# Threshold search of a top-256 selection: bits carried in the threshold, 32 steps written out, six blocks on ScalarE

## The reference, cut to what matters

```
dots  = einsum('bqhe,bke->bqhk', qi, ki)                # 4 index heads of width 64
score = einsum('bqh,bqhk->bqk', wi, relu(dots))
score = where(kpos // 64 <= qpos // 64, score, -1e30)
_, sel = top_k(score, 256)                              # ties: the earlier key wins
...
s = einsum('bqhd,bqjd->bhqj', q, k[sel]) * d**-0.5 + bias
p = softmax(where(valid, s, -1e30))
```

## Time and profile before

| | us |
|---|---|
| runs before, median (lowest, highest) of 3 | 4577.51 (4568.18, 4579.27) |
| profiled execution, time | 4576.58 |
| its span | 4574.8 |
| granted TensorE clock, mean of the span | 0.925 of full |
| TensorE busy in the span | 3894.7 (85%) |
| VectorE busy | 2334.4 (51%) |
| ScalarE busy | 1540.0 (34%) |
| counts of L2329 on VectorE, 340 instructions | 397.8 |
| sign passes of L2369 on ScalarE, 160 instructions | 303.2 |
| matmuls of this stage (cd_pA) | 264.7 + 245.1 |
| rank scans of L2409, 15 instructions | 42.4 |

### The profile page before, as it was taken

One profiled execution on the slowest core, in us unless ns is written; L12 is line 12 of the kernel. 1 busy time (PEld: TensorE's weight loads), 2 busy tenths in 40 slices (PEclk: granted clock), 3 DMA queues, 4 the chain that ended last, 5 costly groups with the idle time before them and its releaser, 6 DMA issues. The chain is left out here.

```text
span 4574.8 us, 52424 instructions
## 1 busy us (share of the span) xinstructions
PE 3894.7 (85%) x18129; PEld 2678.9 (59%) x18129; DVE 2334.4 (51%) x5034; ACT 1540.0 (34%) x2330; POOL 676.9 (15%) x408
## 2 busy tenths in 40 slices
PE   5999999968887999996988787789666489999798
PEld 3789989956664656565856433334344355555376
DVE  6211111157764544532310889999655677766422
ACT  3101001124433343333300778770233233333332
POOL 3100000012112111103400000000111432211133
PEclk9999999989997999998999898889778689999899
DMA  5222122143325222305411111011311311000243
GB/s 185 62 73 73 63 72 70 65 106 87 79 56 107 61 65 65 70 1 185 156 67 52 43 60 46 32 53 62 104 42 44 79 45 32 23 24 5 84 145 131
DMA packets 222646, 328.50 MB, mean 72 GB/s; under 512 B 22240, under 2 KB 129176, under 8 KB 221040
## 3 DMA queue, kind: packets, MB, share of 16 engines
q1 hardware_dynamic: 162768, 216.87, 16.8%
q10 hardware_dynamic: 54432, 91.91, 5.4%
q0 software_dynamic: 5216, 16.70, 1.7%
HBM read 214.42 MB, written 110.99 MB: 71 GB/s over the span
## 5 line engine op out<-in xcount | busy, mean ns | idle before, releaser
L2329 DVE TENSOR_SCALAR_CACHE_REDUCE cd_junk<-score,cd_thr 128x384 bf16<-128x384 f32 (+7 forms) x340 | 397.8, 1236 | 0.1
L1102 DVE TENSOR_REDUCE attB_mx<-attB_p_s 128x1 f32<-128x512 f32 (+2 forms) x360 | 211.2, 608 | 324.4 <-PE attB_p_s L949 207.8
L497 DVE COPY ab_stage<-ab_pA 128x256 f32<-128x256 f32 (+1 forms) x108 | 56.4, 523 | 602.7 <-PE ab_pA L466 572.6
L2369 ACT ACTIVATE cd_scratch<-score,cd_less 128x1664 bf16<-128x1664 f32 (+4 forms) x160 | 303.2, 1895 | 72.4 <-DVE cd_less L2348 67.0
L369 PE MATMUL cd_pA<-hT_cd,cd_W 128*128 128x512 f32 (+1 forms) x640 | 264.7, 578 | 73.4 <-ACT cd_stage L2475 60.9
L464 PE MATMUL ab_pA<-ab_W_hi,h_hi 128*128 128x256 f32 x1088 | 309.0, 284 | 3.2 <-PE ab_pA L466 3.1
L465 PE MATMUL ab_pA<-ab_W_lo,h_hi 128*128 128x256 f32 x1088 | 307.9, 283 | 0.0
L466 PE MATMUL ab_pA<-ab_W_hi,h_lo 128*128 128x256 f32 x1088 | 307.8, 283 | 0.0
L1596 PE MATMUL attD_p_o<-attD_pt,attD_v 128*65 128x512 f32 x548 | 289.4, 609 | 6.7 <-ACT attD_pt L1682 6.7
L1014 PE MATMUL attB_p_o<-attB_pt,attB_v 128*65 128x512 f32 (+3 forms) x656 | 286.3, 525 | 0.0
L495 ACT ACTIVATE ab_stage<-ab_pA 128x256 f32<-128x256 f32 (+1 forms) x108 | 50.1, 464 | 699.5 <-PE ab_pA L466 668.6
(11 more groups left out here) (381 smaller groups left out, 9184.4 us busy)
## 6 DMA issues: line engine op xcount, KB each, us to landing
t_qg<-cd_stage ACTq DMA_DIRECT2D x74, 256.0 KB, 2.0
ab_W_raw<-in_w_ab SPq DMA_DIRECT2D x17, 1024.0 KB, 5.8
mix_o<-t_o SPq DMA_DIRECT2D x34, 512.0 KB, 4.4
t_q<-ab_stage ACTq DMA_DIRECT2D x40, 256.0 KB, 2.0
t_k<-ab_stage ACTq DMA_DIRECT2D x40, 256.0 KB, 2.0
attA_raw<-t_k SPq DMA_DIRECT2D x16, 640.0 KB, 7.3
attA_raw<-t_q SPq DMA_DIRECT2D x16, 640.0 KB, 12.7
attB_raw<-t_k SPq DMA_DIRECT2D x16, 640.0 KB, 7.6
```

Of the source, the lines that this page charges most:

```text
L2329: nc.vector.tensor_scalar(junk[n % 2][:, 0:w], sc[n][:], T[:, n:n + 1], None, op, ALU.add, accum_out=cnt[:, n:n + 1]).then_inc(counted, 1)
L2369: nc.scalar.activation(scratch[:, 0:w], sc[n][:], ACT.Sign, bias=less[:, k:k + 1], accum_out=cnt[:, n:n + 1]).then_inc(signed, 1)
```

## The change

1. **Another state of the search.** `U`, `cand`, `flip`, `bit` and `less` go. The threshold itself (`thr`) carries the bits; for the blocks that ScalarE counts it is the negated threshold, which that engine can add as it is. While the counts run, VectorE prepares `tx`, the threshold with the last try undone and the next bit tried, and once `pred` is known one instruction makes the next threshold. `cnt` and `pred` are double.
2. **32 steps written out** in place of the loops, on VectorE, ScalarE and SP.
3. **Block 2 moves to ScalarE.** VectorE counts blocks 3 to 11, ScalarE 2 and 12 to 16. The order of the blocks is now 3 to 11, 2, 12 to 16 everywhere, also in `index_scores` and in the masks.
4. **Accepted counts are kept** (`kept`, `remember`), and from them comes the room for ties. The 15 counts above the threshold behind the search go; those of the six blocks of ScalarE stay.
5. **The masks are shared.** Whether a rank is within the room is a sign pass on ScalarE (`open_gate`), multiplied on VectorE by the equality and joined with the scores above by a maximum, both on 16-bit data. ScalarE then makes 0/-1e30 of it and writes it over the block's own scores (`leave`).
6. **Units of the projections.** Their DMAs are issued by SP, which also loads the last two weights behind the stores of units 19 and 39. 50 units are emptied inside the search (from its third step on, 0.6 step a unit, the first of a step ahead of ScalarE's fourth pass, a second ahead of the last), four behind it, and 20 behind blocks of masks, one for each six tiles of 128 columns.

The diff, cut to its core:

```diff
-SEL_BLOCKS = list(range(FIRST_SEL, NB))
+N_SIGN = 6
+SEL_BLOCKS = [*range(FIRST_SEL + 1, NB - N_SIGN + 1), FIRST_SEL, *range(NB - N_SIGN + 1, NB)]
...
+    out = [sc[n][:].bitcast(BF16)[:, 0:(b + 1) * P] for n, b in enumerate(SEL_BLOCKS)]
...
     def search(dve):
-        with dve.Fori(0, 32) as i:
-            nc.vector.tensor_tensor(cand[:], U[:], bit[:].broadcast_to([P, NSEL]), ALU.bitwise_or).then_inc(step, 1)
-            to_float(dve, cand, base + 1)
-            nc.vector.tensor_scalar(less[:], T[:, NOWN:NSEL], -1.0, None, ALU.mult).then_inc(step, 1)
-            for n in own:
-                count(dve, n, ALU.is_ge, i * NOWN + n - 1 if n >= 2 else None)
-            nc.vector.tensor_tensor(pred[:], cnt[:], limit[:], ALU.is_ge).then_inc(step, 1)
-            nc.vector.copy_predicated(U[:], pred[:], cand[:]).then_inc(step, 1)
-            nc.vector.tensor_scalar(bit[:], bit[:], 1, None, ALU.logical_shift_right).then_inc(order, 1)
+        for s in range(STEPS):
+            bit = STEPS - 1 - s
+            if s >= 1:
+                dve.wait_ge(turned, s)
+            for n in range(NOWN):
+                nc.vector.tensor_scalar(junk[nth % 2][:, 0:widths[n]], sc[n][:], T[:, n:n + 1], None, ALU.is_ge, ALU.add,
+                                        accum_out=cnt[s % 2][:, n:n + 1]).then_inc(counted, 1)
+                if n == 2 and s >= 1:
+                    undo = 3 * 2 ** (bit - 1) if bit >= 1 else 1
+                    nc.vector.tensor_scalar(tx[:], thr[:], undo, None, ALU.bitwise_xor).then_inc(tried, 1)
+                    remember(dve, s - 1)
+            dve.wait_ge(counted, (s + 1) * NOWN)
+            dve.wait_ge(signed, (s + 1) * N_SIGN)
+            nc.vector.tensor_tensor(pred[s % 2][:], cnt[s % 2][:], limit[:], ALU.is_ge).then_inc(decided, 1)
+            dve.wait_ge(decided, s + 1)
...
+                dve.wait_ge(tried, s + 1)
+                dve.wait_ge(remembered, s)
+                nc.vector.scalar_tensor_tensor(thr[:], pred[s % 2][:], bit, tx[:], ALU.logical_shift_left, ALU.bitwise_xor
+                                               ).then_inc(turned, 1)
+    def remember(dve, s):
+            nc.vector.copy_predicated(kept[:], pred[s % 2][:], cnt[s % 2][:]).then_inc(remembered, 1)
...
     def masks(dve):
-        for n in range(NSEL):
-            count(dve, n, ALU.is_gt, counts + n - 1 if n >= 2 else None)
...
-            nc.vector.scalar_tensor_tensor(keep[:, 0:w], rank[:, 0:w], room[:, n:n + 1], eq[:, 0:w],
-                                           ALU.is_le, ALU.mult).then_inc(order, 1)
-            nc.vector.scalar_tensor_tensor(eq[:, 0:w], sc[n][:], t, keep[:, 0:w], ALU.is_gt, ALU.max
-                                           ).then_inc(order, 1)
-            nc.vector.tensor_scalar(keep[:, 0:w], eq[:, 0:w], -1.0, -NEG, ALU.add, ALU.mult).then_inc(order, 1)
+        ties(0)
+        for n, w in enumerate(widths):
+            if n >= 1:
+                dve.wait_ge(gated, n)
+            nc.vector.tensor_tensor_scan(rank[:, 0:w], junk[n % 2][:, 0:w], zero[:].broadcast_to([P, w]), 0.0,
+                                         ALU.add, ALU.add).then_inc(ranked, 1)
+            if n >= 1:
+                dve.wait_ge(outed, n)
+            nc.vector.tensor_scalar(more[:, 0:w], sc[n][:], T[:, n:n + 1], None, ALU.is_gt).then_inc(greater, 1)
+            dve.wait_ge(ranked, n + 1)
+            nc.vector.tensor_tensor(room[:, n:n + 1], rank[:, w - 1:w], left[:, n:n + 1], ALU.add).then_inc(roomed, 1)
+            if n + 1 < NSEL:
+                ties(n + 1)
+            dve.wait_ge(gated, n + 1)
+            nc.vector.tensor_tensor(gate[:, 0:w], junk[n % 2][:, 0:w], gate[:, 0:w], ALU.mult).then_inc(chosen, 1)
+            nc.vector.tensor_tensor(more[:, 0:w], more[:, 0:w], gate[:, 0:w], ALU.max).then_inc(chosen, 1)
+
+    def open_gate(act, n):
+        act.wait_ge(roomed, n + 1)
+        nc.scalar.activation(gate[:, 0:w], rank[:, 0:w], ACT.Sign, bias=room[:, n:n + 1], scale=-1.0).then_inc(gated, 1)
+
+    def leave(act, n):
+        act.wait_ge(chosen, 2 * n + 2)
+        nc.scalar.activation(out[n], more[:, 0:widths[n]], ACT.Copy, scale=-NEG, bias=NEG).then_inc(outed, 1)
...
 def project_cd(nc, d, hT, sc):
+        STEPS, LEAD, PACE, EARLY, TILES = 32, 2, 0.6, 4, 6
+        while int(LEAD + u * PACE) < STEPS:
+            in_step[int(LEAD + u * PACE)].append(u)
+            u += 1
+        for k in range(EARLY):
+            in_mask[0].append(u)
+            u += 1
+        for n, b in enumerate(SEL_BLOCKS):
+            tiles += b + 1
+            while u < QG2_UNITS and tiles >= TILES:
+                in_mask[n + 1].append(u)
+                u += 1
+                tiles -= TILES
+                def store(u):
+                    sp.wait_ge(ev[u % BANKS], u // BANKS + 2)
+                    sp.dma_start(rows[u * P:(u + 1) * P, :], stage[u % 2][:]).then_inc(stored[u % 2], 16)
+                    if u in last_of:
+                        load(last_of[u] + 2)
+                for s in range(STEPS):
+                    at = {3: in_step[s][0:1], N_SIGN - 1: in_step[s][1:]}
+                    for k in range(N_SIGN):
+                        for u in at.get(k, []):
+                            evacuate(u)
+                        signs(act, s, k)
+                for u in in_mask[0]:
+                    evacuate(u)
+                for n in range(NSEL):
+                    open_gate(act, n)
+                    leave(act, n)
+                    for u in in_mask[n + 1]:
+                        evacuate(u)
```

248 lines of the change are left out of this document (123 added, 125 removed).

## The result

The changed kernel runs in 4514.98 us (median of 4 runs, 4511.64 to 4517.61), the kernel before beside it in 4576.93: ratio 0.9868, 95% interval 0.9851 to 0.9885. It is 62 us faster; 45 were forecast, as 4533 us in a range of 4520 to 4560.

What follows compares the result with a forecast made beforehand. VectorE was taken to bound the search, TensorE the mask part. The search gains 43.6 us, standstill gives back 13 and tail some 11; the stage ends at 3201.6 against 3247.06, 45 us less: 4533 us, range 4520 to 4560.

Steps and rivals of the forecast that it cites:

- Bound and places: Changed stage: VectorE bounds the search step, TensorE the mask part; ScalarE becomes the bound in steps with two evacuations.
- rival B: Search: TensorE falls behind because its short waits keep the clock low; 26 us less, 4551 us; 12%.
- C: Search: ScalarE's step is longer than summed by 0.5 us a step, 16 us in all, 4549 us; 9%.
- TensorE's standstill: Start of the mask part: TensorE stands still some 13 us, as unit 54 is emptied only behind the second block.
- The price of a step: Search: 12.33 us with two evacuations, 11.84 with one, 11.79 for VectorE's chain; 388.6 us in all.
- VectorE's own step: Search: VectorE's counts, small operations and decision chain sum to 11.79 us, with 0.25 for two small operations between counts.
- Masks' part and tail: Behind the search: TensorE bounds the masks and ends at 3187; the tail adds 11.6 us, then 3.05 to the next stage.
- D: Search: evacuations waiting for TensorE inside a step hold the threshold; 38 us slower, 4615 us; 4%.
- E: Changed stage: search edits save little and standstill and tail eat it; within 0.3%, which is 14 us; 5%.
- The products of two 16-bit tensors: Mask blocks: product and maximum taken as 1.3 us at 2176 columns; 2 us less to 5 us more on the path.
- Other stages at 0: index_scores: the new block order leaves its units the same, put at 0, within 1 us either way.
- The stretch behind the stage put at 0: From the next stage's first instruction to the span's end: forecast as before, 1327.7 us, no gain.

Runs made afterwards that it cites:

- The recounts put back: Changed kernel with the fifteen dropped is_gt counts run again on VectorE ahead of the mask blocks, results unused: 4542.5 us, ratio 0.9921 to the kernel before.
- The pace experiment: Changed kernel with 54 instead of 50 units emptied in the search, six right behind it, one per ten tiles: 4491.8 us, ratio 0.9818 to the kernel before.
- the loop written out: Kernel before, with only VectorE's 32 search steps written out instead of looped: 4560.1 us, ratio 0.9967.
- the copy on the path: Changed kernel with the two small operations between decision and new threshold instead of between counts: 4529.8 us, ratio 0.9902 to the kernel before.
- the kernel with five blocks: Changed kernel with five blocks on ScalarE instead of six, and the block order of before: 4526.1 us, ratio 0.9887 to the kernel before.
- the wait of attention D: GpSimd builds near masks only after VectorE's query split, added to both kernels: before 4516.5 us, changed 4463.7 us.
- one line of numbers: Changed kernel with eight units emptied right behind the search instead of four, then one per nine tiles instead of six: 4497.6 us, ratio 0.9824 to the kernel before.

## Why the prediction was wrong, step by step

- **Bound and places: right.** TensorE, tied to the steps before, is freed by faster steps; the evacuations did not wait in the search, TensorE came back to a clock of 0.98 over the search (rival B refuted; its 0.77 was one stretch of a search with a mean of 0.89), and the step never came near 12.8 us (C refuted). The recounts put back show that what stands ahead of the blocks sets TensorE's standstill.
- **The price of a step: wrong, and this is the step that failed** in the changed stage. Forecast were 12.33 us with two evacuations and 11.84 with one; measured 12.01 and 11.67. Over 20 and 10 steps that is 6.4 + 1.7 = 8.1 us of the 8.3 missed in the search. Three terms were mis-sized:
  - an evacuation adds 0.35 us, not 0.49. I had taken its length against a gap of 0.12, which is 0.46 and not the 0.49 that went into the sum: that slip alone is 0.06 of a double step, 1.5 us of the search. And the next pass starts 0.47 behind it (3008.04 to 3008.51), 0.1 before it ends, as it starts itself 0.1 before the accumulator read ends. Two: 0.28. The pace experiment has the same 0.35.
  - the new threshold follows 0.21 behind the decision, not 0.32. I had read 0.32 from a row whose second operation is a predicated copy. In the loop written out that distance stayed 0.32, and with the copy on the path the operation behind it waited 0.31: the tenth belongs to the predicated copy, on either side of it, not to the number of waits. 0.11.
  - against these, the decision starts 0.10 behind the late accumulator read's end (3015.19 to 3015.29), not 0.02. -0.08. This goes with the writing out: 0.03 in both profiles of the kernel before, 0.10 to 0.11 in the one whose loop alone was written out. Why, no run shows.
- **VectorE's own step: not the bound at all.** The two small operations cost 0.08 each, not 0.25 together. By the rows it would be 10.88 + 0.16 + 0.13 + 0.21 + 0.21 = 11.59, or 11.49 with the 0.03 to the decision that a written-out loop shows in place of 0.13, and ScalarE's 11.31 + 0.35 with one evacuation is 11.66: VectorE waited for ScalarE in 30 steps, not only in those with two.
- **Masks' part and tail: right.** 167.5 us against 168.0. The standstill is 8.2 us and not 13, since TensorE filled its four banks 31.4 us behind the first recount instead of 27.4 and went on after 39.6 instead of 41.0 (3067.47). Only the moment when it goes on sets its end: the last evacuation is 152.8 behind the recount (forecast 153.4), and the tail is 14.66 (11.6 + 3.05). Rivals D and E are refuted: nothing waited in the steps, and no gain was lost but the two forecast.
- **The products of two 16-bit tensors**: 1.29 us at 2176 columns, as taken (1.3), and 1.23 at 2048, as the Trainium skill (VectorE: DVE Perf Modes, The perf-mode tier table) gives it.
- **Other stages at 0: nearly right.** From the first matmul of index_scores to the first count it is 124.2 us in the mean of nine profiles with the new block order (123.5 to 124.8) and 125.4 in five with the old one (124.7 to 125.9, the kernel with five blocks among them): 1.3 us less, where 0 within 1 was said. The first count itself starts between 2643.3 and 2651.2 us, and most of that scatter is older than the changed code.
- **The stretch behind the stage put at 0: wrong, too.** I had one profiled execution and took its stretch behind the stage for constant; it measured 9.3 us less. By the medians the change brought 61.9 us, with the wait of attention D in both kernels 52.9. With either miss alone, 8.3 or 9.3 us under 4533, the time would lie inside the range, at about 4525 or 4524. It took both, and no run shows the second to be a property of the change: with the wait in both kernels the stretch is 5.6 us longer in the changed one (1270.1 against 1264.5). So that part of the miss is the luck of the executions, as far as is known. Left open: whether the changed kernel meets the short case more often than the kernel before. Without the wait, the sixth split was short in 5 of 7 profiles with the new search and long in all 3 with the old one, too few to tell, and nothing in the changed stage was shown to lead there.

## What to carry to other kernels

A change is priced by the latencies between operations, so read each from a row with the same second operation, the same engine and the same kind of loop: 0.1 to 0.14 us a term, three terms, 30 steps made 8 us. Where work of a second engine is tied to the program order of a third, its standstill and the order of the last few pieces are worth as much as the loop that was made faster: here 22.5 us came back by one line of numbers. Look for an operation whose longest time is far from its median (1.22 and 9.2 us for the split, 0.50 and 5.84 for the cast): the wait that shortened both was the largest gain in this kernel, and it lay in no stage that the change touched. And when a remedy brings over three times what its reason allows, as here (57 us where 3 to 18 were expected), look for where the time came back: it was at another operation.
